# Where weights are stationary: three 256-column matmuls onto one half bank instead of one of 512 and one of 256

## The reference, cut to what matters

```python
h = rmsnorm(x, norm_g)
z = h @ w_in                        # 256 x 2048 @ 2048 x 6144
q_a, k_a, v_a, g_a, u_p, g_p, q_m, g_m = jnp.split(z, IN_OFFSETS, axis=-1)
mk, mv = jnp.split(rmsnorm(mem, mem_norm_g) @ w_mem_kv, 2, axis=-1)   # 2048 x 1024
y = concat([moba_attention(q_a, k_a, v_a) * silu(g_a),
            multiscale_pool(u_p) * silu(g_p),
            memory_attention(q_m, mk, mv) * silu(g_m)]) @ w_out       # 2048 x 2048
out = rmsnorm(x + y, final_norm_g)
```

## Time and profile before

| | |
|---|---|
| median of three runs | 443.48 us (443.45 to 443.78) |
| the profiled execution, device time | 443.56 us |
| its span in the trace | 441.5 us |
| mean granted TensorE clock | 0.994 |
| PE busy | 429.7 us, 97% of the span, 2252 matmul records |
| PEld busy (weight loads) | 368.4 us, 83% |
| DVE busy | 266.2 us, 60% |
| ACT busy | 219.8 us, 50% |

### The profile page before, as it was taken

How to read it: one execution, slowest core, us unless ns; L and a number is a source line. 1 busy time by engine, 2 the same in 40 slices (tenths; PEclk the granted TensorE clock), 3 DMA queues, 4 the chain that set the end, 5 groups by cost and what they waited for, 6 DMA issues and landing times.

```text
span 441.5 us, 6001 instructions
## 1 busy us (share of the span) xinstructions
PE 429.7 (97%) x2252; PEld 368.4 (83%) x2252; DVE 266.2 (60%) x292; ACT 219.8 (50%) x297; POOL 26.5 (6%) x48
## 2 busy tenths in 40 slices
PE   7999999999999999999999999999999999999992
PEld 6788888888888888888888888888888888888881
DVE  3856775545464667646557677857664575658522
ACT  5855684744343434646454544355464544347311
POOL 1000000000000020000020200002000101121200
PEclk9999999999999999999999999999999999999997
DMA  8999858655555556442728855455646257655022
GB/s 286 405 402 413 333 187 335 232 187 184 191 175 194 178 185 191 140 146 95 238 91 307 354 180 183 153 213 161 221 131 203 68 181 229 196 184 192 0 96 96
DMA packets 25369, 89.77 MB, mean 203 GB/s; under 512 B 2944, under 2 KB 3072, under 8 KB 24448
## 3 DMA queue, kind: packets, MB, share of 16 engines
q1 hardware_dynamic: 24048, 81.56, 54.7%
q10 hardware_dynamic: 1296, 7.86, 4.4%
HBM read 87.31 MB, written 2.10 MB: 203 GB/s over the span
## 4 chain that ended last, share of the span: by engine, by line
PE 92%; issue 2%; DMA 2%; SPq 1%; DVE 1%; ACT 0%; POOLq 0%; POOL 0%; DVEq 0%; ACTq 0%
PE ps L350 36%; PE ps L353 17%; PE ps L374 11%; PE ps L372 11%; PE ps L373 11%; DMA w_raw<-in_w_mem_kv 2%; PE ps L359 1%; PE ps L389 1%; PE ps L420 1%; PE ps L416 1%; PE ps L384 1%; PE ps L404 1%; PE ps L421 0%; PE ps L388 0%; PE ps L400 0%
## 5 line engine op out<-in xcount | busy, mean ns | idle before, releaser
L685 DVE TENSOR_TENSOR w_lo<-w_raw,w_hi 128x1024 fp32r<-128x1024 f32 x138 | 175.2, 1282 | 121.7 <-ACT w_hi L509 121.4
L350 PE MATMUL ps<-xT,w_hi 128*128 128x512 f32 x640 | 222.7, 397 | 0.0
L509 ACT ACTIVATE w_hi<-w_raw 128x1024 fp32r<-128x1024 f32 x138 | 144.7, 1058 | 132.6 <-PE ps L353 78.4
L353 PE MATMUL ps<-xT,w_lo 128*128 128x256 f32 x600 | 168.2, 280 | 0.0
L350 PEld LDWEIGHTS ps<-xT,w_hi 128*128 128x128 f32 x640 | 119.5, 188 | 27.0
L353 PEld LDWEIGHTS ps<-xT,w_lo 128*128 128x128 f32 x600 | 113.4, 189 | 0.1
L372 PE MATMUL ps<-w_hi,yT 128*128 128x512 f32 x112 | 43.6, 390 | 0.0
L374 PE MATMUL ps<-w_hi,yT 128*128 128x512 f32 x112 | 43.6, 389 | 0.0
L373 PE MATMUL ps<-w_lo,yT 128*128 128x512 f32 x112 | 43.6, 389 | 0.0
L372 PE MATMUL ps<-w_hi,xT 128*128 128x512 f32 x64 | 25.5, 399 | 0.0
L350 PE MATMUL ps<-memT,w_hi 128*128 128x512 f32 x64 | 22.8, 403 | 2.7 <-DVE w_lo L699 1.8
(11 more groups left out here) (129 smaller groups left out, 384.0 us busy)
## 6 DMA issues: line engine op xcount, KB each, us to landing
w_raw<-in_w_in SPq DMA_DIRECT2D x96, 512.0 KB, 4.2
w_raw<-in_w_out SPq DMA_DIRECT2D x32, 512.0 KB, 4.3
w_raw<-in_w_mem_kv SPq DMA_DIRECT2D x14, 512.0 KB, 12.0
x_t_raw<-in_x_t SPq DMA_DIRECT2D x8, 256.0 KB, 13.2
rows<-in_x ACTq DMA_DIRECT2D x2, 1024.0 KB, 10.4
rows<-in_mem ACTq DMA_DIRECT2D x2, 1024.0 KB, 8.9
x_res<-in_x ACTq DMA_DIRECT2D x2, 1024.0 KB, 7.5
mem_raw<-in_mem_head SPq DMA_DIRECT2D x3, 512.0 KB, 8.8
```

What stands on the lines that cost most here:

```text
L350: pe.matmul(acc, hi[:, t, f * P:(f + 1) * P], moving[:, kt], start=(kt == 0), stop=(kt == KT - 1), skip_group_check=True)
L353: m = pe.matmul(acc[:, 0:S], lo[:, t, f * P:(f + 1) * P], moving[:, kt, 0], start=False, stop=(kt == KT - 1), skip_group_check=True)
L509: act.activation(halves_of(n)[0], w_raw[:, n % RAW], ACT.Copy).then_inc(hi_done, 1)
L685: dve.tensor_tensor(lo, w_raw[:, n % RAW], hi.bitcast(F32), ALU.subtract).then_inc(lo_done, 1)
```

## The change

`rows_are_features` multiplies with 256 columns at a time. For each `kt` and `f` there are now three matmuls in a row onto the first half of bank `f`: high weights by high activations, high weights by low activations, low weights by high activations. The second half of the bank isn't used. The separate loop for the first block is gone; the wait for the very first low weights (`first_lo`) stands in the first triple. `part_b` is no longer written at the end of a group (the tile stays, for the tanh of the gates), its semaphore is gone, and so are ACT's copy and the waits in front of it. DVE takes the whole sum out of the bank in one instruction: with the group's factor alone, or with the factor and `x_rstd`.

```diff
+        def features_of(g, f):
+            return ps[:, bank0(g) + f, 0:S]
...
                     for f in range(NF):
-                        acc = ps[:, bank0(g) + f, :]
-                        pe.matmul(acc, hi[:, t, f * P:(f + 1) * P], moving[:, kt], start=(kt == 0),
-                                  stop=(kt == KT - 1), skip_group_check=True)
-                        if kt:
-                            m = pe.matmul(acc[:, 0:S], lo[:, t, f * P:(f + 1) * P], moving[:, kt, 0],
-                                          start=False, stop=(kt == KT - 1), skip_group_check=True)
-                    if n == 0 and t == 0:
-                        pe.wait_ge(first_lo, 1)
-                    if kt == 0:
-                        for f in range(NF):
-                            pe.matmul(ps[:, bank0(g) + f, 0:S], lo[:, t, f * P:(f + 1) * P], moving[:, kt, 0],
-                                      start=False, stop=False, skip_group_check=True)
+                        acc = features_of(g, f)
+                        own = slice(f * P, (f + 1) * P)
+                        pe.matmul(acc, hi[:, t, own], moving[:, kt, 0], start=(kt == 0), stop=False)
+                        pe.matmul(acc, hi[:, t, own], moving[:, kt, 1], start=False, stop=False)
+                        if n == 0 and t == 0 and f == 0:
+                            pe.wait_ge(first_lo, 1)
+                        m = pe.matmul(acc, lo[:, t, own], moving[:, kt, 0], start=False, stop=(kt == KT - 1))
...
-                if a == PPG - 1 and g < OUT0 and g not in TOKENS_ON_ROWS:
-                    act.wait_ge(piece_used, n + 1)
-                    if g >= 1:
-                        act.wait_ge(evacuated, g)
-                    if g - 1 in GATES:
-                        act.wait_ge(y_ready, GATES.index(g - 1) + 1)
-                    act.activation(part_b[:, :, :], ps[:, bank0(g):bank0(g) + NF, S:2 * S], ACT.Copy,
-                                   scale=FACTOR.get(g, 1.0)).then_inc(part_b_ready, 1)
...
-                dve.wait_ge(part_b_ready, sum(i not in TOKENS_ON_ROWS for i in range(g + 1)))
                 if g in GATES and g != GA0:
                     dve.wait_ge(y_lo, GATES.index(g))
-                hi_part = ps[:, bank0(g):bank0(g) + NF, 0:S]
-                m = dve.scalar_tensor_tensor(out=dst[:, :, :], in0=hi_part, scalar=FACTOR.get(g, 1.0),
-                                             in1=part_b[:, :, :], op0=ALU.mult, op1=ALU.add)
-                if g not in (MK, Q0, Q1, QM):
-                    settle(m)
-                    m = dve.tensor_tensor(dst[:, :, :], dst[:, :, :], x_rstd[:, :, :].to_broadcast([P, NF, S]), ALU.mult)
+                done = ps[:, bank0(g):bank0(g) + NF, 0:S]
+                if g in (MK, Q0, Q1, QM):
+                    m = dve.tensor_scalar(dst[:, :, :], done, FACTOR.get(g, 1.0), None, ALU.mult)
+                else:
+                    m = dve.scalar_tensor_tensor(out=dst[:, :, :], in0=done, scalar=FACTOR.get(g, 1.0),
+                                                 in1=x_rstd[:, :, :].to_broadcast([P, NF, S]), op0=ALU.mult, op1=ALU.mult)
```

More of the change, by code:

```diff
@@ L182, in build @@
         mv_scaled = sem("mv_scaled")
-        part_b_ready = sem("part_b_ready")
         evacuated = sem("evacuated")
```

## The result

The changed kernel takes 449.93 us (median, 449.86 to 450.13), beside 443.63 us of the kernel before on the same chip: a ratio of 1.0145, with a 95% interval of 1.0131 to 1.0159. It is slower, by 6.3 us. The prediction had 447.8 us, with a range of 440 to 453.

A forecast was written before the change was run, and what follows sets the result against it. The prediction took TensorE's distances between matmul starts to bound the kernel: 443.56 us profiled plus 4.2 us for 680 triples at 6.2 ns more each, all else at nothing, gives 447.8 us, range 440 to 453.

The forecast's parts named there:

- The bound: After 17.73 us TensorE never waits for another engine; time is the sum of distances between matmul starts.
- the covers: Work saved on ACT and DVE and the moved first wait are hidden behind TensorE or idle time: nothing.
- the sign: Whole kernel: slower with chance 0.67, same 0.15, faster 0.18.
- the forecast's own band: Triple of 352 to 358.5 ns, kernel time 444.8 to 449.3 us, chance 0.45.
- The emptying: Group ends: fewer ACT copies and DVE instructions free banks some 2.3 us earlier, wanted only 22 us later; costed at nothing.
- The wait for the first low weights: Kernel start: it stands after 512 columns instead of 2048; 1.77 us of idle time take up any delay.
- the price of the triple: Three 256-column matmuls at L359's 118.75 ns each: 356.3 ns against 350.1 for the pair, 6.2 ns more.
- the term of 4.2 us: Matmuls after 17.73 us: 680 triples, each 6.2 ns dearer than the pair it replaces.
- A fixed price for each matmul: Cost beyond columns doesn't depend on their number: triple 360 to 370 ns, time 450.5 to 456.9 us; chance 0.2.
- The faster rival: Uniform stream of equal matmuls onto one bank settles at 113 ns each: 436.7 us, 6.9 less; chance 0.17.
- The bank and the place: Three sums in a row onto the same 256 columns cost nothing; changing bank each matmul may cost something.
- The sequencer: TensorE's sequencer becomes the bound with six instructions a triple: at 62 ns each, 372 ns, 458.5 us; chance 0.05.

The follow-up runs named there:

- run 1: Kernel before with only its 512-column matmul cut into two of 256, one onto each half of the bank, old emptying kept: 450.01 us, ratio 1.0145.
- Run 4: Kernel before with four 512-column matmuls, then the four 256-column ones, in every block instead of only a group's first: 443.68 us, ratio 1.0005.
- run 3: Changed kernel with its three matmuls reordered so that each goes to another bank than the one before it: 449.93 us, ratio 1.0147.
- run 6: Kernel before with its 512-column matmul cut into 384 and 128 columns, the 256-column one kept: 482.0 us, ratio 1.0879.
- run 2: Kernel before with the 256-column matmul of the low weights cut into two of 128, the 512-column one whole: 517.2 us, ratio 1.1655.

## Why the prediction was right, and what was mis-sized

**The bound, the covers and the sign** held. TensorE's distances set the time, no new wait came, the clock didn't move. But 449.93 us lies above the forecast's own band of 444.8 to 449.3, and 360.0 ns above its 352 to 358.5: the value that was favoured missed, and it is the width of the range, kept for the rivals, that holds the result. The emptying was costed at nothing, and run 1 beside the changed kernel shows that it is: with ACT's copies and with DVE's second instructions the time is the same within 0.1 us. The wait for the first low weights cost nothing to be seen (the idle time after it went from 1.8 to 2.0 us).

**The mis-sized term** is the price of the triple, "A triple by this price is 356.3 ns". It measured 360.0 in the ten groups, so the term of 4.2 us is 6.4 by these groups of the trace, 6.6 with MK, and 6.3 by the runs. In MK it measured 353.3, below the forecast. The reason given for the choice, that L359 is the same instruction with short neighbours at full clock, overlooked that only three of its four distances lie between short matmuls, and that a run of four is not yet a stream. Run 4 shows the consequence: in a mixture, 117.5 ns for a short one goes with 232.5 for a long one, 5.8 more than a long one costs among its like. The two rows had to be priced together: the earlier trace rows give 0.925 + 0.475 us for 3072 columns in eight matmuls, 1280 ns of columns and 15.0 for each matmul, and three of these make a triple of 365, on the other side of the truth.

**The rivals.** "A fixed price for each matmul" was the right mechanism for the ten groups: its lower end, 360.3 ns and 450.5 us, is within 0.6 us of the result, which falls into the gap between it and the forecast. It got chance 0.2 because 118.75 is less than 120; the equality of 13.3 in V0's stream and 13.4 in K0's pair was the better evidence, as it came from whole periods and not from a part of one. It was not clean evidence either: K1's pair gave 16.6, and MV's stream, not read then, gives 20.0. The range's upper end was also miscounted: 453 us takes in about 0.4 of the way from 450.5 to 456.9, not two thirds. The faster rival failed on its own premise: equal matmuls onto one bank settle, but at 120 ns, or 117.8 in MK, and not at 113; MK's 113 came from three distances. The bank and the place are of no account (runs 1 and 3). The sequencer was never near (2.2 us ahead), which the bound from the earlier trace rows allowed.

**The floor** was not among the rivals. It doesn't decide here, 0.11 against 0.12 us, but one step further, at 128 columns, it takes over: runs 6 and 2 are 38 and 74 us slower than the kernel before, six and twelve times what the change cost.

**Still open**: what part of the 13.3 ns is the load. Two narrow loads of three save 10 to 13.3 of a triple's 40 ns in the ten groups and 2 of its 33 in MK; halving them again saves nothing in the ten groups and 11 in MK. Nor is it shown what chooses between 346.7 and 353 ns for the same pairs; only that both occur without the first block's own order, and that four other orders have one pace alone. And it isn't shown why MK's and MV's streams differ from those of the other groups.

## What to carry to other kernels

Where TensorE is the bound, count matmuls as well as columns: here each fp32r matmul with its own 128x128 load cost 13.3 ns beyond its columns in ten groups of eleven, so cutting a 512-column matmul in two costs that once more, however idle the engines are that the cut relieves. Price a new stream from whole periods of a settled one, in more than one stretch of the program, and fit columns and count together; the distance of one matmul in a mixture isn't its cost. Below 256 columns the load's own 0.11 us takes over.

## What the runs showed of the hardware that I had not expected

Uniform streams of fp32r matmuls mostly settled at columns / 2.4 GHz + 13.3 ns: 120.0 for 256, 173.4 for 384, 226.7 for 512. Two settled elsewhere at the same granted clock: 117.8 for 256 columns in MK, 233.3 for 512 in MV. A mixture costs 0 to 7 ns a pair more than two such prices (22.19 to 22.6 us for 64 pairs), and with pairs the same program does the one in some groups and the other in others. Where 128-column matmuls stood, loads of 128 columns started 0.11 us apart. Loads of 64 columns in two of three matmuls took the triple from 360 to 346.7 or 350 ns, and loads of 32 columns no further, except in MK (340.5).
